# An encoder step on one core: the norm's root moved from the projections' input to their sums

## The reference, cut to what matters

```
def rmsnorm(x, g):
    y = x32 * lax.rsqrt(jnp.mean(x32 * x32, axis=-1, keepdims=True) + EPS)
    return y * g

for l in range(2):
    h = rmsnorm(x, norm_mix_g[l])
    ua|va|q|k|v|cin|gb|gc|gates = h @ w_in[l]       # 512 columns each, gates 3072
    vn = rmsnorm(gelu(va), g_v)
    A = gelu(ua) * (masked ws . vn + bs)            # over 128-token chunks
    B = band attention of q, k, v with a relative bias
    C = gb * causal_conv3(gc * cin)
    x = x + W_out(sum_b sigmoid(gates_b) * (branch_b @ W_branch_b))
    h = rmsnorm(x, norm_ffn_g[l])
    x = x + (W2(silu(h @ W1) * (h @ W3)) if l == 0 else top-2-of-8 experts(h))
y = rmsnorm(x, final_norm_g)
```

## Time and profile before

| | |
|---|---|
| three runs | 1896.94, 1897.38, 1898.65 us |
| median | 1897.38 us |
| the profiled execution | 1896.74 us, its span 1894.8 us |
| TensorE busy | 1809.1 us of the span |
| VectorE, ScalarE, GpSimd busy | 1378.6, 1086.6, 35.6 us |
| read and written | 477.38 MB, 7.88 MB |

### The profile page before, as it was taken

How to read it: one execution, slowest core, us unless ns; L and a number is a source line. 1 busy time by engine, 2 the same in 40 slices (tenths; PEclk the granted TensorE clock), 3 DMA queues, 4 the chain that set the end, 5 groups by cost and what they waited for, 6 DMA issues and landing times.

```text
span 1894.8 us, 27667 instructions
## 1 busy us (share of the span) xinstructions
PE 1809.1 (95%) x10646; PEld 1614.3 (85%) x10646; DVE 1378.6 (73%) x1424; ACT 1086.6 (57%) x1067; POOL 35.6 (2%) x64
## 2 busy tenths in 40 slices
PE   5998998999989989988999999999999999999995
PEld 5998998999979989977888888888888888888884
DVE  4475556666654855566889889898898897988984
ACT  4353344333343634444777777777777777777773
POOL 2101000000000000000000000000000000000000
PEclk8999999999999999988999999999999999999998
DMA  9755553454524524444999999999999999999990
GB/s 327 222 154 154 176 164 126 157 177 154 177 93 158 165 84 161 151 150 182 381 371 353 338 352 351 365 364 345 333 355 356 371 346 325 369 349 371 355 368 32
DMA packets 253014, 486.98 MB, mean 257 GB/s; under 512 B 8000, under 2 KB 97120, under 8 KB 252640
## 3 DMA queue, kind: packets, MB, share of 16 engines
q1 hardware_dynamic: 247504, 466.64, 70.2%
q0 software_dynamic: 4336, 17.46, 2.8%
q10 hardware_dynamic: 1056, 1.18, 0.2%
HBM read 477.38 MB, written 7.88 MB: 256 GB/s over the span
## 4 chain that ended last, share of the span: by engine, by line
issue 65%; PE 31%; DVE 2%; DMA 1%; ACT 1%; POOL 0%; ACTq 0%; POOLq 0%; DVEq 0%
PE psum L1701 8%; PE psum L1702 8%; PE psum L1703 8%; PE psum L1570 1%; PE psum L1571 1%; PE psum L1572 1%; DMA x<-in_x_t 1%; DVE h L1034 1%; PE psum L1677 0%; PE psum L1676 0%; PE psum L1675 0%; PE psum L1550 0%; DVE rstd L1031 0%; DVE w_lo L1044 0%; ACT w_hi L767 0%
## 5 line engine op out<-in xcount | busy, mean ns | idle before, releaser
L1304 DVE TENSOR_TENSOR e_lo<-ring,e_hi 128x2048 fp32r<-128x2048 f32 x224 | 512.4, 2292 | 94.0 <-ACT e_hi L934 93.5
L934 ACT ACTIVATE e_hi<-ring 128x2048 fp32r<-128x2048 f32 x224 | 429.4, 1918 | 186.9 <-PE psum L1822 93.6
L1044 DVE TENSOR_TENSOR w_lo<-ring,w_hi 128x1024 fp32r<-128x1024 f32 x218 | 266.9, 1230 | 220.0 <-ACT w_hi L767 219.8
L767 ACT ACTIVATE w_hi<-ring 128x1024 fp32r<-128x1024 f32 x218 | 230.2, 1057 | 262.4 <-PE psum L1703 196.9
L1820 PE MATMUL psum<-e_hi,he_hi 128*128 128x512 f32 x896 | 356.2, 398 | 0.2 <-ACT he_lo L940 0.2
L1822 PE MATMUL psum<-e_hi,he_lo 128*128 128x512 f32 x896 | 351.9, 393 | 0.0
L1821 PE MATMUL psum<-e_lo,he_hi 128*128 128x512 f32 x896 | 351.4, 392 | 0.0
L1701 PE MATMUL psum<-h_hi,w_hi 128*128 128x288 f32 x1120 | 332.6, 297 | 7.7 <-DVE h_lo L1050 6.6
L1702 PE MATMUL psum<-h_lo,w_hi 128*128 128x288 f32 x1120 | 331.0, 296 | 0.0
L1703 PE MATMUL psum<-h_hi,w_lo 128*128 128x288 f32 x1120 | 330.0, 295 | 0.0
L1304 DVE TENSOR_TENSOR e_lo<-spare,e_hi 128x2048 fp32r<-128x2048 f32 x112 | 256.4, 2289 | 36.1 <-ACT e_hi L934 36.0
(11 more groups left out here) (280 smaller groups left out, 2192.4 us busy)
## 6 DMA issues: line engine op xcount, KB each, us to landing
ring<-in_e_w SPq DMA_DIRECT2D x224, 1024.0 KB, 5.8
spare<-in_e_w SPq DMA_DIRECT2D x112, 1024.0 KB, 5.5
ring<-in_w_in SPq DMA_DIRECT2D x56, 1024.0 KB, 5.1
ring<-in_w SPq DMA_DIRECT2D x33, 1024.0 KB, 5.3
ring<-in_w_branch SPq DMA_DIRECT2D x12, 1024.0 KB, 5.0
ring<-in_w_out SPq DMA_DIRECT2D x8, 1024.0 KB, 4.9
bias_ext<-attn POOLq DMA_DIRECT2D x2, 2048.0 KB, 9.1
bias<-bias_ext POOLq DMA_DIRECT2D x2, 1536.0 KB, 13.6
```

Source lines behind the costliest of these rows:

```text
L767: nc.scalar.activation(dst, src, ACT.Copy).then_inc(rounded, 1)
L934: nc.scalar.activation(e_hi[c % BUFS][:, :], expert_ring[s][:, 0:PIECE_W], ACT.Copy).then_inc(piece_rounded, 1)
L1044: nc.vector.tensor_tensor(low, src, high.bitcast(f32), ALU.subtract).then_inc(split, 1)
L1304: nc.vector.tensor_tensor(e_lo[buf][:, :], expert_ring[s][:, 0:PIECE_W], e_hi[buf][:, :].bitcast(f32), ALU.subtract).then_inc(piece_split, 1)
```

## The change

Norms 0, 1 and 2 change; 3 and 4 are left as they were. x times the norm's weights (not times rstd) is split and goes into the projections, and each sum is multiplied by rstd when it leaves its bank; gc*cin is multiplied by rstd squared. The squares are added on VectorE, and TensorE sums them over the partitions with one matmul, which stands behind the second chunk. v and va are computed like the others, with the weight chunk stationary, and are then transposed by TensorE to tokens on partitions. The ScalarE functions that took sums from PSUM (tanh, silu, gelu) now take what VectorE has scaled into SBUF. Cut to its core:

```diff
 def mixer_groups(l):
-    g = [("norm", 2 * l)]
-    g += [("v", l, h, n) for h in range(2) for n in range(3)]
-    g += [("q", l, j) for j in range(BT)] + [("k", l, j) for j in range(BT)]
-    g += [("ua", l, j) for j in range(BT)]
-    g += [("va", l, h, n) for h in range(2) for n in range(3)]
+    g = [("v", l, 0), ("v", l, 1), ("norm", 2 * l), ("v", l, 2), ("v", l, 3)]
+    g += [("q", l, 0), ("q", l, 1)] + [("vt", l, n) for n in range(3)] + [("q", l, 2), ("q", l, 3)]
+    g += [(s, l, j) for s in ("k", "ua", "va") for j in range(BT)]
     g += [("s", l, h) for h in range(HEADS)] + [("s2", l, r) for r in range(2)]
+    g += [("vat", l, n) for n in range(3)]
...
@@ ScalarE @@
+            def x_high(n, k):
+                ...
+                nc.scalar.activation(h_hi[:, k, :], x[:, k, :], ACT.Copy, scale=vec[:, gain:gain + 1]).then_inc(h_rounded, 1)
             for l in range(2):
                 first = MIXER_FIRST[l]
                 if l:
                     for c in range(3):
                         round_lead(first + c)
+                    for k in range(DT):
+                        x_high(n, k)
+                        square(n, k)
+                else:
+                    for k in range(DT):
+                        x_high(n, k)
+                        if k % 4 == 3:
+                            round_lead(first + k // 4)
+                    for k in range(DT):
+                        square(n, k)
+                    round_lead(first + 2)
                 round_lead(first + 3)
+                for j in range(BT):
+                    round_lead(CHUNK_OF[("q", l, j)])
+                    if j == 1:
+                        root(n)
...
+                for j in range(BT):
+                    round_lead(CHUNK_OF[("cin", l, j)])
+                rows_evacuated("vat", l, vg, vg_ready, ACT.Gelu_apprx_tanh)
...
-                    evacuate(("gate", l, g), gate[:, g % 4, :], P, TOK, gate_ready, ACT.Tanh, scale=0.5)
                     round_lead(gates + 6 * (g // 4) + g % 4 + CHUNKS)
+                    act.wait_ge(gate_scaled, 24 * l + g + 1)
+                    nc.scalar.activation(gate[:, g % 4, :], gate[:, g % 4, :], ACT.Tanh, scale=0.5).then_inc(gate_ready, 1)
...
+                    for k in range(DT):
+                        if k < CHUNKS:
+                            round_lead(OUT_FIRST[l] + CHUNKS + k)
+                        elif k < DT - 1:
+                            round_lead(DENSE_FIRST + k - CHUNKS)
+                        x_high(1, k)
+                        square(1, k)
...
@@ VectorE @@
+            def x_low(n, k):
+                ...
+                nc.vector.scalar_tensor_tensor(out=h_lo[:, k, :], in0=x[:, k, :], scalar=vec[:, gain:gain + 1],
+                                               in1=h_hi[:, k, :].bitcast(f32), op0=ALU.mult, op1=ALU.subtract
+                                               ).then_inc(h_low_ready, 1)
+            def sum_squares(n):
+                dve.wait_ge(squared, DT * (n + 1))
+                done(nc.vector.tensor_tensor(sq[:, 0:4, :], sq[:, 0:4, :], sq[:, 4:8, :], ALU.add))
+                ...
+                nc.vector.tensor_tensor(sq[:, 0, :], sq[:, 0, :], sq[:, 1, :], ALU.add).then_inc(sums_ready, 1)
+            def scaled(name, dst, done):
+                full(name)
+                nc.vector.tensor_tensor(dst, bank(name), rstd[:, :], ALU.mult).then_inc(done, 1)
...
             for l in range(2):
+                for k in range(BT if l else 0, DT):
+                    x_low(n, k)
+                    if l == 0 and k % 4 == 3:
+                        low_lead(first + k // 4)
+                sum_squares(n)
+                for c in range(3 if l else 2, CHUNKS + 2):
+                    low_lead(first + c)
+                rstd_of(n)
...
+                for s, dst, done_by in (("q", q_t, qk_ready), ("k", key_t, qk_ready), ("ua", a_t, ua_scaled), ("va", va_t, va_scaled)):
                     for j in range(BT):
+                        low_lead(CHUNK_OF[(s, l, j)] + CHUNKS)
+                        scaled((s, l, j), dst[:, j, :], done_by)
...
-                    nc.vector.tensor_copy(z[:, j, 2:2 + SEQ], tmp[:, j % 2, 0:SEQ])
+                    nc.vector.tensor_tensor(z[:, j, 2:2 + SEQ], tmp[:, j % 2, 0:SEQ], rstd2[:, 0:SEQ], ALU.mult)
...
-                    full(("gb", l, j))
-                    p = bank(("gb", l, j))
-                    nc.vector.tensor_tensor(c_t[:, j, 0:SEQ], y[:, 0:SEQ], p[:, 0:SEQ], ALU.mult)
+                    scaled(("gb", l, j), c_t[:, j, :], dve_step)
+                    settle()
+                    nc.vector.tensor_tensor(c_t[:, j, 0:SEQ], y[:, 0:SEQ], c_t[:, j, 0:SEQ], ALU.mult)
...
                             low_lead(first + CHUNKS + c)
+                            scaled(("gate", l, g), gate[:, c, :], gate_scaled)
...
@@ VectorE, the dense block: four of the x_low(2, k) ahead of the last w2 sums @@
+                        if c == end + CHUNKS - 1:
+                            for k in range(BT):
+                                x_low(2, k)
...
@@ TensorE @@
+            def turn_rows(seg, l, src, ready):
+                pe.wait_ge(ready, BT * (l + 1))
+                for n, (t0, rows) in enumerate(TILES):
+                    take((seg, l, n))
+                    for j in range(BT):
+                        ins = nc.tensor.transpose(bank((seg, l, n), rows, HALF)[:, j * P:(j + 1) * P], src[:, j, t0:t0 + rows],
+                                                  ident[:, :])
+                    give(ins)
             for l in range(2):
-                mean(NORM_OF_LAYER[l])
-                rows_of("v", l)
-                features("q", l)
+                features("v", l, range(2))
+                mean_sum(NORM_OF_LAYER[l])
+                features("v", l, range(2, BT))
+                features("q", l, range(2))
+                turn_rows("vt", l, v_t, v_scaled)
+                features("q", l, range(2, BT))
                 features("k", l)
                 features("ua", l)
-                rows_of("va", l)
+                features("va", l)
                 scores(l)
+                turn_rows("vat", l, va_t, va_scaled)
                 features("cin", l)
```

More of the change, by code:

```diff
@@ L175, in mixer_groups @@
     g += [("out", l, j) for j in range(DT)]
-    g += [("norm", 2 * l + 1)]
     return g
@@ L214, in number_groups @@
         if u < DENSE_UNITS:
-            g.add(groups_in(("dense", u)))
+            names = groups_in(("dense", u))
+            g.add(names[0:2] + [("norm", 1)] + names[2:4] if u == 0 else names)
         if u:
             g.add(groups_out(("dense", u - 1)))
-    g.add(mixer_groups(1))
+    g.add(mixer_groups(1) + [("norm", 3)])
     g.add([("htok", n, hf) for hf in range(2) for n in range(3)] + [("logits",), ("counts",)])
+    g.next = 0
     g.add([("norm", 4)])
@@ L813, in _ @@
                         round_lead(first + c)
-                squares(NORM_OF_LAYER[l])
-                if l == 0:
-                    for c in range(3):
-                        round_lead(first + c)
-                root(NORM_OF_LAYER[l])
-                round_h(NORM_OF_LAYER[l])
-                round_lead(first + 3)
-                for hf in range(2):
-                    for part in range(2):
-                        round_lead(CHUNK_AT[("q", l, hf), part])
-                    rows_evacuated("v", l, hf, v_tok, v_ready, ACT.Copy)
@@ L1008, in _ @@
             y_rounded(last_pair, 1)
-            squares(4, last_pair)
+            for k in range(DT):
+                square(4, k, last_pair)
             root(4)
@@ L1064, in after_dense @@
                 (w, u), part = LEAD_ORDER[c]
+                dve.wait_ge(chunk_used, c + 1)
+                t = KB * (u % 2) + part
                 if w == "w1":
-                    return
-                dve.wait_ge(chunk_used, c + 1)
-                if w == "w3":
+                    scaled(("a", ("dense", u), part), silu[:, t, :], a_scaled)
+                elif w == "w3":
+                    scaled(("g", ("dense", u), part), hid[:, t, :], dve_step)
+                    steps[0] += 1
+                    settle()
                     dve.wait_ge(silu_ready, KB * u + part + 1)
-                    t = KB * (u % 2) + part
-                    nc.vector.tensor_tensor(hid[:, t, :], silu[:, t, :], bank(("g", ("dense", u), part)),
-                                            ALU.mult).then_inc(hid_ready, 1)
+                    nc.vector.tensor_tensor(hid[:, t, :], silu[:, t, :], hid[:, t, :], ALU.mult).then_inc(hid_ready, 1)
                     if (u, part) == (0, KB - 1):
@@ L1551, in mean, with mean_sum @@
                 give(ins)
[L1553 to L1573 removed]
+            def mean_sum(n):
+                take(("norm", n))
+                pe.wait_ge(sums_ready, n + 1)
+                give(nc.tensor.matmul(bank(("norm", n)), mean_w[:, :], sq[:, 0, :], start=True, stop=True))
+            def turn_rows(seg, l, src, ready):
```

(12 more changed lines are left out.)

227 lines of the change are left out of this document (108 added, 119 removed).

## The result

The changed kernel takes 1872.71 us in the median of 4 runs (1871.49 to 1875.19), the kernel before 1898.02 beside it: a ratio of 0.9868, 95% interval 0.9852 to 0.9883. The forecast was 1868.3, within 1859 to 1877: the sign and the range hold, and the gain is 25.3 us where 29.1 were summed.

What follows compares the result with a forecast made beforehand. TensorE, busy 1809 of 1895 us, was taken as the bound. Terms -11.9 - 12.2 - 14.2 + 5.4 + 3.8 = -29.1 gave 1867.7 us in the profiled execution, 1868.3 as median; forecast 1864 to 1871, wider range 1859 to 1877.

Steps and rivals of the forecast that it cites:

- The dense start: Dense block's start, norm 1: the root leaves TensorE's path and hides beside later chunks, -11.9 us.
- Layer 1 and the start: Layer 1 up to its first score, -16.5 us; the kernel's start up to the first score, -18.5 us.
- C: Norms hidden less: late x_low(7), mean's sum or slot gives 3 to 9 us back, 1871 to 1878; chance 0.12.
- F: Held weights save nothing, a chunk of v still takes 4.23 us: +17, 1885; chance 0.02.
- The score stretch: First score to gc, each layer: va's transpositions delay ScalarE's chain and gc by 7.0 us; less va's gain of 4.3, +2.7.
- Rival B: Score stretch hides, or convolution's extra fits TensorE's slack: 5 to 11 us of losses go, 1858 to 1863; chance 0.17.
- rival E: Table switches cost 2.66 us, so two behind gelu hold gc 2.8 us longer per layer: 1874; chance 0.01.
- The convolution: Before attention, each layer: scaling and hand-over add 0.5 us to each of four tiles on VectorE, +1.9.
- The gates: Gate blocks: 48 scalings of 0.455 us on VectorE hide beside TensorE's chunks, costed at 0.
- Attention: Attention in both layers: no change in length, 0.
- rival A: New pauses before gc and in the start cost the clock, 1.7 us each: 1872 to 1874; chance 0.2.

Runs made afterwards that it cites:

- the second profiled execution: The changed kernel itself, unedited, run once more: median 1871.92 us, ratio 0.9856 against the kernel before; its profiled execution took 1874.41 us.

## Why the prediction was right, and where it was off

**The dense start (-11.9; -11.7).** Right in size and steps: the last `h_lo` 1.8 us behind w_out (forecast 1.6), root and reciprocal hidden. With the root back on the path the stretch is 10.3 longer, and TensorE's own sums would add their 3.5.

**Layer 1 and the start (-16.5, -18.5; -16.3, -18.4).** Right, va's gain included (4.3 in the sum; 4.2 by the traces, 17.0 less 12.8). Layer 1's first chunk was to end 2.4 us late behind ScalarE's x_high; it ended 2.5 late (a chunk of 3.2 before the mean's product at 525.07, where the dense block ends at 516.1), 1.2 of it the wait for `h_lo` seen above. v's last chunk was to end at 29.4 and ended at 29.65; the next chunks follow 3.20 apart, the held weights' pace:

```profile
29.65 1.06 ACT L769 ACTIVATE w_hi<-ring 128x1024 fp32r<-128x1024 f32 x1 [2.12 <-PE psum L1752]
32.85 1.06 ACT L769 ACTIVATE w_hi<-ring 128x1024 fp32r<-128x1024 f32 x1 [2.14 <-PE psum L1752]
```

Rivals C and F did not occur.

**The score stretch (+7.0; +7.5, twice).** Right in its mechanism, a little short: gelu ended 10.5 us behind the first score, not 10.05. The bank of head 4 was read 8.7 us behind it, as summed; but at half clock the last four transpositions took 1.0 us where four take 0.6 at full clock; all twelve of va took 3.3, v's twelve 1.5. Cin, too, began at half clock and ended later than summed, so the pause before gc was to be 3.2 and was 2.4 and 1.2; gc's start hangs on ScalarE all the same. No long pause stands ahead of this half clock: in layer 0 TensorE had waited 0.27 and 0.46 us. Its small multiplications now last 10.1 us without a chunk between them, in the kernel before 6.2; whether that is the cause no run tests by itself. Rival B is out.

The table loads followed the row: exponentials begin 1.30 us after the load at 96.42. The 2.66 us for a switch that the Trainium skill states (ScalarE: Activation LUTs, What ACT_TABLE_LOAD costs) show nowhere in this stretch, and rival E is out.

**The convolution (+1.9; +1.9, twice).** Right as a term: 14.7 us for 12.8, wait 5.6. Its price in the whole is not shown: in both profiled executions without the scaling the wait shrinks by 1.9 and attention is 1.5 to 4.5 us longer, for a reason that stays open.

**The gates (0; 0.0).** Right, with room: twice the scaling costs nothing beside the gates, and 0.7 in w_out.

**Attention (0; +1.5 and +0.5).** This is the step that failed: no term of the sum held half clock. The prediction counted it as rival A alone, and only behind the *new* pauses, those before gc and in the start. But attention's half clock was in the trace of before too: it took 17.2 and 16.7 us there, and takes 15.6 without a pause. Over all profiled executions with a pause ahead of it, attention was 16.7 to 21.7 behind 3.7 to 5.6, so 1 to 6 us more. What sets it within that span the runs don't settle: the longer pause doesn't make the longer half clock (21.7 behind 3.7, 17.2 behind 5.6), and the changed kernel gave 18.7 and 17.2, then 17.2 and 16.8. So the 2.0 here are partly chance: in the second profiled execution only 0.1 of them is left, and half clock takes 1.5 in gc and 1.5 in v instead.

So rival A, held at 0.2 and priced at 1872 to 1874, is the nearest to what happened, at four places of which it named one, gc's start in the second execution; the score stretch, attention and layer 1's v it didn't name.

## What to carry to other kernels

A factor that is the same for a whole sum can wait until the sum leaves its bank, and the chain that makes it then hides behind the sums; what is lost is one pass per result on an engine with room. Then look at the blocks of small work between large multiplications: here they were worth more (32 to 33 us) than the whole change (25), because TensorE waits in and behind such blocks and half clock comes with them, 1 to 6 us of it in attention. Weave such work between the chunks, or at least do early what the next stage waits for.

## What the runs showed of the hardware

How long half clock lasts is not set by the pause ahead of it alone. In attention it lasted 4.5 and 3.4 us behind 3.7 in the kernel before, 12.8, 8.7, 16.3 and 16.4 behind the same 3.7 without gb's scaling, and 3.5 to 12.3 behind 5.6; in the dense chunks it lasted 5.1 behind 8.3. At the end of the scores it came for 6.8 us with no wait over 0.6 us just ahead of it.

Two heads' scores, on rows 0 to 63 and 64 to 127, cost between chunks what one costs, 1.04 us. The Trainium skill says as much (TensorEngine Tiling (Array Packing), Key Properties: different tiles can multiply in parallel), and the rows of one head and of two above agree.

VectorE slows beside a copy on POOL. The split of a chunk takes 1.23 us, in 218 of them on average, and here, in the changed kernel, 2.27:

```profile
L1061 DVE TENSOR_TENSOR w_lo<-ring,w_hi 128x1024 fp32r<-128x1024 f32 x218 | 266.4, 1228 | 169.8 <-ACT w_hi L769 168.0
```
```profile
36.44 1.89 POOL L702 COPY attn<-attn 128x2040 f32<-128x2040 f32 x1 [9.02 <-DMA attn<-in_bias_rev]
...
37.14 2.27 DVE L1061 TENSOR_TENSOR w_lo<-ring,w_hi 128x1024 fp32r<-128x1024 f32 x1 [1.60 <-ACT w_hi L769]
```

The copy has 1.19 us left when the split begins, and the split is 1.04 longer. The Trainium skill has the rule (SBUF — State Buffer, Who interferes with whom: a VectorE instruction with two inputs in SBUF contends with a GpSimd one that reads there), and the trace agrees. It stood off TensorE's path here.
